# Two transformer blocks on one core: first loads spread out, masks made by GpSimd, memory norm one group later, two norms summed by halves

## The reference, cut to what matters

```python
for layer in range(2):                                   # first block
    h = rms_norm(x, norm_g[layer])
    sb_q, sb_k, sb_v, sb_g, mb_q, mb_k, mb_v, mb_g, mem_q, mem_g = split(h @ w_in[layer])
    o_sb  = stick_breaking_attention(...) * silu(sb_g)   # 6 heads
    o_mb  = softmax attention, causal, with rotary (...) * silu(mb_g)   # 6 heads
    m     = rms_norm(mem, mem_norm_g[layer])             # 256 memory rows of 1024
    mk, mv = split(m @ w_mem_kv[layer])
    o_mem = softmax(mem_q @ mk.T / 8) @ mv * silu(mem_g) # 4 heads
    x = x + concat(o_sb, o_mb, o_mem) @ w_out[layer]
x = rms_norm(x, final_norm_g)
# second block: 16 meta tokens in front of the 256
u = rms_norm(h, pre_mix_gain); proj = u @ w_in_2
merged = g_swa * (o_swa @ w_branch_swa) + g_diff * (o_diff @ w_branch_diff)
h = h + rms_norm(merged @ w_out_2, post_mix_gain)
u = rms_norm(h, pre_ffn_gain); gate, up = split(u @ w_ffn_in)
h = h + rms_norm((silu(gate) * up) @ w_ffn_out, post_ffn_gain)
```

## Time and profile before

| | |
|---|---|
| median of 3 runs | 888.32 us (886.84 to 890.65) |
| the profiled execution | 884.68 us, its span 882.9 us |
| PE busy | 829.7 us, 94% of the span |
| DVE, ACT, POOL busy | 554.1, 471.4, 122.4 us |
| mean granted clock of TensorE | 0.979 of full speed |
| transfers | 138.13 MB, 156 GB/s over the span |

### The profile page before, as it was taken

How to read it: one execution, slowest core, us unless ns; L and a number is a source line. 1 busy time by engine, 2 the same in 40 slices (tenths; PEclk the granted TensorE clock), 3 DMA queues, 4 the chain that set the end, 5 groups by cost and what they waited for, 6 DMA issues and landing times.

```text
span 882.9 us, 13033 instructions
## 1 busy us (share of the span) xinstructions
PE 829.7 (94%) x4350; PEld 684.0 (77%) x4350; DVE 554.1 (63%) x854; ACT 471.4 (53%) x962; POOL 122.4 (14%) x198
## 2 busy tenths in 40 slices
PE   7799999999999999699989999999998999999995
PEld 5678878777776787589878888888886788888884
DVE  5476667676777676756555665766566555455453
ACT  5476565375775554645555566555535544344343
POOL 0200121000232310153222524200000000000000
PEclk9999999999999999799999999999999899999999
DMA  9944543466676454652212434546664556656641
GB/s 268 268 139 128 146 120 122 141 177 205 193 216 184 139 161 120 174 143 83 63 55 71 127 108 126 166 145 208 204 202 138 186 182 193 209 155 197 207 137 48
DMA packets 147584, 138.13 MB, mean 156 GB/s; under 512 B 15184, under 2 KB 115680, under 8 KB 147520
## 3 DMA queue, kind: packets, MB, share of 16 engines
q1 hardware_dynamic: 145440, 130.21, 48.5%
q0 software_dynamic: 2080, 7.09, 2.8%
HBM read 136.22 MB, written 1.05 MB: 155 GB/s over the span
## 4 chain that ended last, share of the span: by engine, by line
PE 45%; ACT 4%; DVE 3%; issue 1%; ACTq 0%; DVEq 0%
PE psum L1059 38%; PE psum L1025 3%; PE psum L1142 2%; ACT probs L1406 2%; ACT w_hi L1294 1%; PE psum L1252 1%; DVE stats L1571 1%; DVE w_lo L1461 1%; PE psum L1255 1%; ACT xn L1316 0%; ACT gtmp L1436 0%; DVE xn L1500 0%; DVE x L1504 0%; ACT hstat L1439 0%; DVE o_st L1625 0%
## 5 line engine op out<-in xcount | busy, mean ns | idle before, releaser
L1461 DVE TENSOR_TENSOR w_lo<-raw,w_hi 128x1024 fp32r<-128x1024 f32 (+1 forms) x254 | 296.9, 1183 | 139.1 <-ACT w_hi L1294 82.3
L1294 ACT ACTIVATE w_hi<-raw 128x1024 fp32r<-128x1024 f32 (+1 forms) x254 | 253.0, 1015 | 70.7 <-PE psum L1059 47.2
L1059 PE MATMUL psum<-w_hi,h_hi 128*128 128x512 f32 (+1 forms) x656 | 262.8, 401 | 13.0 <-DVE h_lo L1510 10.3
L1059 PE MATMUL psum<-w_lo,h_hi 128*128 128x512 f32 (+1 forms) x656 | 248.8, 379 | 0.0
L1059 PE MATMUL psum<-w_hi,h_lo 128*128 128x512 f32 (+1 forms) x656 | 248.5, 379 | 0.0
L1059 PEld LDWEIGHTS psum<-w_hi,h_hi 128*128 128x128 f32 x656 | 125.7, 192 | 36.0 <-issue 15.8
L1059 PEld LDWEIGHTS psum<-w_lo,h_hi 128*128 128x128 f32 x656 | 125.1, 191 | 19.8
L1059 PEld LDWEIGHTS psum<-w_hi,h_lo 128*128 128x128 f32 x656 | 126.0, 192 | 16.2
L1406 ACT ACTIVATE probs<-psum,stats 128x272 f32<-128x272 f32 (+2 forms) x104 | 47.6, 467 | 87.4 <-DVE stats L1563 30.2
L1059 PE MATMUL psum<-w_hi,m_hi 128*128 128x512 f32 x152 | 60.0, 395 | 2.4 <-DVE m_lo L1510 1.7
L1059 PE MATMUL psum<-w_lo,m_hi 128*128 128x512 f32 x152 | 59.2, 390 | 0.0
(11 more groups left out here) (158 smaller groups left out, 1053.0 us busy)
## 6 DMA issues: line engine op xcount, KB each, us to landing
raw<-in_w_in SPq DMA_DIRECT2D x112, 256.0 KB, 3.5
raw<-in_w_in SPq DMA_DIRECT2D x44, 512.0 KB, 4.4
raw<-in_w_ffn_in SPq DMA_DIRECT2D x88, 256.0 KB, 3.9
raw<-in_w_out SPq DMA_DIRECT2D x24, 512.0 KB, 3.4
raw<-in_w_in SPq DMA_DIRECT2D x64, 192.0 KB, 2.7
raw<-in_w_ffn_out SPq DMA_DIRECT2D x22, 512.0 KB, 4.6
raw<-in_w_mem_kv SPq DMA_DIRECT2D x8, 512.0 KB, 3.8
raw<-in_w_branch_swa SPq DMA_DIRECT2D x8, 512.0 KB, 3.3
```

The costliest lines, as they stand in the source:

```text
L1059: last = nc.tensor.matmul(psum[:, bank, 0:n], sx[name][:, c, t * P:(t + 1) * P], wx[:, u["slot"], kk, 0:n], start=u["first"] and kk == 0 a ...
L1294: nc.scalar.activation(w_hi[:, u["slot"], :, 0:n], raw[:, u["raw"], :, 0:n], ACT.Copy)\
L1461: nc.vector.tensor_tensor(w_lo[:, u["slot"], :, 0:n], raw[:, u["raw"], :, 0:n], w_hi[:, u["slot"], :, 0:n].bitcast(F32), ALU.subtract)\
```

## The change

Five things change. First loads: the table `cf` is loaded in two other pieces (identity and triangle first, 128 KB; the rotary tables after unit 11 instead of unit 5, and with them no block of ones), the mask table is no longer loaded, GpSimd makes the masks from identity and triangle; its own loads (a gain, the memory rows in two halves, the small vectors, the next gain) wait for the 5th, 7th, 9th, 12th and 15th weight split, where before all of them waited for the 6th. Order of the groups: mb0 of layer 0 moves ahead of mkv and mem, with the memory norm beside it; `turn_mix` of the memory heads comes 9.75 units after their group instead of 11.5; `small` moves to layer 1. Between the blocks: the norm of the second token tile comes behind the transposes of the first. The two `addnorm`s: each bank is squared by itself (`half`), DVE multiplies it by the gain meanwhile, and the sum of the two halves gives the root; then one pass of DVE scales and adds. The diff, cut to its core:

```diff
-                out=(5.75, 6.75, 7.75, 8.75), turn_mix=(11.5,)),
+                out=(5.75, 6.75, 7.75, 8.75), turn_mix=(9.75,)),
...
-            side(head_group(layer, "sb", 1), {1: [("masks", None)], 3: [("small", None)]})
-            side(head_group(layer, "sb", 2), {0: mem_norm, 1: turns[:1], 2: turns[1:3], 3: turns[3:]})
+            side(head_group(layer, "sb", 1), {0: [("masks", None)]})
+            side(head_group(layer, "sb", 2), {})
+            side(head_group(layer, "mb", 0), {0: mem_norm, 1: turns[:1], 2: turns[1:3], 3: turns[3:]})
             turn_keys = memory_keys(layer, {})
             side(head_group(layer, "mem", 0), {0: [turn_keys]})
+            mem_norm, turns = memory_norm()
+            side(head_group(layer, "mb", 1), {0: mem_norm})
+            side(head_group(layer, "mb", 2), {k: [turn] for k, turn in enumerate(turns)})
...
-            side(meta_group(4), {0: [after[0], final[1]], 2: [after[1]]})
+            side(meta_group(4), {0: [after[0], final[1]]})
             line.extend(norm_turns("xn", "h", 0))
+            line.append(after[1])
...
-    tile_by_tile(a[2:] + b[2:], [post[0], pre[0]])
+    for t, name in enumerate(("unit_a", "unit_b")):
+        for g, units in zip(wo2, (a, b)):
+            line.extend((name, u) for u in units[2:])
+            line.append(half(post, g, t))
+        if t == 0:
+            line.extend([post[0], pre[0]])
     line.extend(norm_turns("xn", "h", 0) + [post[1]])
...
-            sp.dma_start(cf[:, 0:C_TRI], cf_dram[:, 0:C_TRI]).then_inc(s_ident, 16)
+            sp.dma_start(cf[:, 0:C_ONE], cf_dram[:, 0:C_ONE]).then_inc(s_ident, 16)
...
-                elif u["u"] == NRAW + 1:
-                    sp.dma_start(cf[:, C_TRI:C_END], cf_dram[:, C_TRI:C_END]).then_inc(s_const, 16)
-
-                    sp.dma_start(mask_in, cb_dram).then_inc(s_const, 16)
+                elif u["u"] == 11:
+                    sp.dma_start(cf[:, C_COS1:C_END], cf_dram[:, C_COS1:C_END]).then_inc(s_const, 16)
...
-            pool.wait_ge(hi_ready, NRAW + 2)
+            pool.wait_ge(s_ident, 16)
+            ident, below = cf[:, C_ID:C_ID + P], cf[:, C_TRI:C_TRI + P]
+            nc.gpsimd.memset(cf[:, C_ONE:C_ONE + P], -1.0)
+            nc.gpsimd.tensor_copy(cb[:, B_ID:B_ID + P], ident)
+            nc.gpsimd.tensor_scalar(cb[:, B_SB:B_SB + P], below, -NEG, None, ALU.mult)
+            nc.gpsimd.tensor_scalar(cb[:, B_LOW:B_LOW + P], below, NEG, NEG, ALU.mult, ALU.add)
+            link(nc.gpsimd.tensor_tensor(rtmp[:, 0, 0:P], below, ident, ALU.add))
+            nc.gpsimd.tensor_scalar(cb[:, B_UP:B_UP + P], rtmp[:, 0, 0:P], -NEG, None, ALU.mult)\
+                .then_inc(const_done, 1)
...
+            pool.wait_ge(hi_ready, 5)
             load_gain(pool, 1)
-            pool.dma_start(mem_v, A["mem"][0].rearrange("(t p) d -> p t d", p=P)).then_inc(s_mem, 16)
+            for t in range(NT):
+                pool.wait_ge(hi_ready, 7 + 2 * t)
+                pool.dma_start(mem_v[:, t, :], A["mem"][0, t * P:(t + 1) * P, :]).then_inc(s_mem, 16)
+            pool.wait_ge(hi_ready, 12)
...
-            pool.wait_ge(s_const, 32)
+            pool.wait_ge(hi_ready, 15)
+            pool.wait_ge(s_const, 16)
...
+                elif what == "half":
+                    g, t = s["g"], s["t"]
+                    wait(act, s["ready"])
+                    nc.scalar.activation(p_t[:, g["n"], :], psum[:, g["banks"][t], :], ACT.Square, scale=D ** -0.5,
+                                         accum_out=hsum[:, 2 * t + g["n"]:2 * t + g["n"] + 1]).then_inc(half_summed, 1)
+                elif what == "addnorm":
...
+                    link(nc.scalar.activation(more, more, ACT.Identity, bias=eps_col[:, :]))
+                    link(nc.scalar.activation(ss, ss, ACT.Ln, bias=more))
+                    nc.scalar.activation(rs, ss, ACT.Exp, scale=-0.5).then_inc(rstd_ready, 1)
...
-                elif what == "masks":
-                    dve.wait_ge(s_const, 32)
-                    nc.vector.tensor_copy(cb[:], mask_in).then_inc(const_done, 1)
...
+                elif what == "half":
+                    g, t = s["g"], s["t"]
+                    dve.wait_ge(*gain_use[i][1:])
+                    dve.wait_ge(half_summed, s["half"])
+                    at = slice(g["n"] * 512, (g["n"] + 1) * 512)
+                    link(nc.vector.tensor_tensor(xn[:, t, at], psum[:, g["banks"][t], :],
+                                                 gain[:, gain_use[i][0], at], ALU.mult))
+                elif what == "addnorm":
...
+                    nc.vector.scalar_tensor_tensor(out=x[:, t, :], in0=xn[:, t, :], scalar=nstat[:, 16 + c:17 + c],
+                                                   in1=x[:, t, :], op0=ALU.mult, op1=ALU.add).then_inc(norm_done, 1)
...
-                    if what == "addnorm":
-                        link(last)
-                        last = nc.vector.tensor_tensor(x[:, t, :], x[:, t, :], xn[:, t, :], ALU.add)
```

More of the change, by code:

```diff
@@ L118, in __init__ @@
                                     "his", "gated", "roped", "pts", "blends", "norms", "rstd", "norm_done",
-                                    "groups", "silus", "turns"), 0)
+                                    "groups", "silus", "turns", "halves"), 0)
     def next(self, name, n=1):
@@ L369, in number @@
                 outs_of_pt.append(s["o"] + 1)
+        elif what == "half":
+            s["ready"] = g["t_done"][s["t"]]
+            s["half"] = pl.next("halves")
         elif what in ("norm", "addnorm", "metanorm"):
@@ L374, in number @@
                 N["done"] = []
+            if what == "addnorm":
+                s["half"] = pl.count["halves"]
             if what == "metanorm":
                 s["ready"] = ("s_meta", 16)
-            elif what == "addnorm":
-                s["ready"] = product_done[t]
-            else:
+            elif what == "norm":
                 s["ready"] = (mem_ready if N["source"] == "mem" else x_ready)[t]
@@ L435, in norm_turns, with half @@
         return [("turn_norm", dict(source=source, dest=dest, t=t, c=c)) for c in range(0, KC, 4)]
-    def tile_by_tile(units, between=()):
-        line.extend(("unit_a", u) for u in units)
-        line.extend(between)
-        line.extend(("unit_b", u) for u in units)
+    def half(N, g, t):
+        return ("half", dict(norm=N[0][1]["norm"], g=g, t=t))
     w1 = [W["w_in"][layer] for layer in range(DEPTH)]
@@ L519, in make_plan @@
             with_meta(head_group(layer, "mem", 0, (0, 1)), 2, {0: [("rope_meta", dict(n=1))]})
-        for p in range(3):
-            extra = {}
-            if layer == 0 and p == 0:
-                mem_norm, turns = memory_norm()
-                extra = {0: mem_norm}
-            elif layer == 0 and p == 1:
-                extra = {k: [turn] for k, turn in enumerate(turns)}
-            if layer == 1 and p == 0:
-                with_meta(head_group(layer, "mb", p, (0, 1)), 3, {0: [("rope_meta", dict(n=2))]})
-            elif layer == 1:
-                side(head_group(layer, "mb", p, (2, 3) if p == 1 else (0, 1)), extra)
-            else:
-                side(head_group(layer, "mb", p), extra)
+            with_meta(head_group(layer, "mb", 0, (0, 1)), 3, {0: [("rope_meta", dict(n=2))]})
+            side(head_group(layer, "mb", 1, (2, 3)), {0: [("small", None)]})
+            side(head_group(layer, "mb", 2, (0, 1)), {})
         outs = [pl.group("wo", banks() if layer == 0 else ((2, 3), (0, 1))[n], units_of(
@@ L633, in make_plan @@
     last_outs = outs_of(nf - 1)
-    line.extend(("unit_a", u) for u in last_outs)
     final = norm("addnorm")
-    line.append(final[0])
-    line.extend(("unit_b", u) for u in held + last_outs)
-    line.append(final[1])
+    for t, name in enumerate(("unit_a", "unit_b")):
+        if t:
+            line.extend((name, u) for u in held)
+        for g, u in zip(fo, last_outs):
+            line.extend([(name, u), half(final, g, t)])
+        line.append(final[t])
     pl.steps = lay_out(line)
@@ L793, in build @@
         for i, (what, s) in enumerate(STEPS):
-            if what in ("norm", "metanorm", "addnorm") and s["t"] > 0:
+            if what in ("norm", "metanorm", "addnorm", "half") and "gain" in s["norm"]:
                 gain_use[i] = s["norm"]["gain"]
@@ L797, in build @@
                 continue
-            if what in ("norm", "metanorm", "addnorm") or (what == "evac" and s["g"]["kind"] == "gates"
+            if what in ("norm", "metanorm", "half") or (what == "evac" and s["g"]["kind"] == "gates"
                                                           and s["g"]["n"] % 2 == 0 and s["t"] == 0):
@@ L1301, in _ @@
                     split(s)
[L1302 removed]
+                elif what == "half":
[4 more added lines that the diff above has]
+                elif what == "addnorm":
+                    N, t = s["norm"], s["t"]
+                    c = 4 * (N["n"] % 4) + 2 * t
```

(6 more changed lines are left out.)

50 lines of the change are left out of this document (19 added, 31 removed).

## The result

The changed kernel takes 882.16 us (median of 18 runs, 880.32 to 887.23), the kernel before 888.38 (18 runs). The ratio is 0.9948 with a 95% interval of 0.9929 to 0.9968: 2.8 to 6.3 us less. Forecast were 882.5 us. Timed once more beside later experiments (e5), it took 881.92 against 888.51, ratio 0.9932 (0.9911 to 0.9953).

The account below looks back on a forecast made before the run. PE, busy 94% of the span, was taken as the bound, so other engines cost only where PE waits. Terms summed to -5.84 us, from 888.32 to 882.5; the 8-in-10 range was 878.8 to 888.8.

Parts of the forecast that it names:

- Start: Up to the first matmul: larger first table costs 0.25 us, GpSimd's masks beside `w_lo` 0.1, together +0.35.
- Mask wait: PE's wait for `cb` near 32 us goes, since GpSimd makes the masks long before: -1.62 us.
- late weights: PE's 3.10 us wait at 43.46: 0.73 MB less in GpSimd's loads lets weights arrive earlier, -2.7 us.
- Low clock at 44 us: Behind the wait at 43.46, 4 us at clock 0.61 should stay high without that wait: -1.56 us.
- Between the blocks: PE's 5.09 us wait for the first `h_lo` shortens as the second tile's norm moves behind it: -1.3 us.
- After `w_out_2`: Wait for `xn` falls to 0.8 us, but the second tile's multiplications delay `h_lo`: +0.1 in all.
- End: The shortened norm chain behind the last matmul, exposed with only the store after it: -1.4 us.
- the starvation moves forward: Rival, 890.4 us, chance 0.07: three early 0.52 MB GpSimd loads hold up SP's weights, 5.9 us together.
- The weights stay late: Rival, 886.8 us, chance 0.17: the savings of 2.7 and 1.56 us do not come.
- Each new wait brings a low clock: Rival, 885.6 us, chance 0.16: (a) and (b) cost 2 x 1.56 us more.
- (a): Layer 0, memory keys' transposes: PE waits until DVE has read a bank of the two-bank ring, +0.6 us.
- (b): Layer 0, memory heads' output transposes right ahead of the unit needing their `mix` parts: PE waits, +1.69 us.

Follow-up runs that it names:

- e5: The changed kernel once more, unchanged, timed beside e6 and e7: 881.92 us against 888.51 for the kernel before, ratio 0.9932.
- e8: Changed kernel with the mask table again, loaded by SP and cast by DVE, GpSimd's loads still spread: 887.57 us, ratio 1.0011 to the kernel before.
- e2: Changed kernel with all of GpSimd's loads issued behind the 6th weight split again, masks still by GpSimd: 891.32 us, ratio 1.0018 to the kernel before.
- e6: Changed kernel with GpSimd's large loads (gain, memory rows) behind the 6th weight split, small vectors still behind the 12th: 883.35 us, ratio 0.9949.
- e7: Changed kernel with only the small vectors moved ahead, behind the 6th weight split: 886.99 us, ratio 0.9984 to the kernel before.
- e3: Changed kernel with the second tile's halves at `w_out_2` behind the first tile's `h_hi` and `h_lo`: 878.56 us, ratio 0.9891.
- e9: Kernel before with one edit, small vectors and the gain behind them waiting for the 12th weight split instead of the 6th: 881.92 us, ratio 0.9944.

## Why the prediction was right

The time was forecast to 0.3 us by nine terms. Six came out singly (start, both new waits of layer 0, the chain between the blocks, `w_out_2`, end), two only as a sum and for a wrong cause, and the ninth, the low clock, can't be read from one pair of traces. So the closeness of the total is in part luck.

- *Start, +0.35*: in the first pair of traces the first matmul came at 12.01 instead of 12.07, as if nothing were lost. Over all traces it came at 11.92 to 12.13 in ten with the larger table, and at 12.07, 11.34 and 11.62 in the three with the smaller one, on average 0.36 later. Masks on GpSimd are not the reason, as e8, which makes none there, starts at 12.06. The loss that I allowed for beside `w_lo` had hardly a place to come from: the last mask step ends at 10.06, 0.03 us after the first `w_lo` begins (0.25 in e5), and that `w_lo` takes the 1.23 us that it took before:

```profile
9.53 0.53 POOL L907 TENSOR_SCALAR cb<-rtmp 128x128 bf16<-128x128 f32 x1
10.03 1.23 DVE L1472 TENSOR_TENSOR w_lo<-raw,w_hi 128x1024 fp32r<-128x1024 f32 x1 [2.26 <-ACT w_hi L1294]
```

- *Mask wait, -1.62, and late weights, -2.7*: the sum of -4.3 was right (the first `sbt` matmul came 4.8 earlier), the parts were wrong. They are not two terms: e2 keeps one edit and PE waits 6.20, e8 keeps the other and PE waits 4.13. The cause was wrong too. "0.73 MB less at 268 GB/s" took bytes for the price; e6 moves 1.57 MB for 1.4 us, e7 0.2 MB for 5.1. That the step gave the right figure is luck: the 0.73 MB that I took out of the stretch are the small vectors (0.2) and a gain (0.52), and I priced every byte alike, where the 0.2 did most of it.
- *Low clock at 44 us, -1.56*: gone in both traces of after. But I took one trace's low stretches as given. They come behind other waits in other runs, so the term is a mean over runs; from 10 and 13 to 9 and 9 it is 2.5 x 1.7 = 4.3 us, an upper bound, since some of these stretches lie where PE waits anyway.
- *Layer 0, +0.6 and +1.69*: 0.77 and 1.50 measured. I did not see the 0.39 for a row of the memory norm, nor the 0.18 more at 72 us.
- *Between the blocks, -1.3*: from the start of the last matmul of the meta tokens to the first unit it took 6.06 us instead of 7.45 in the first pair of traces, 6.03 instead of 7.45 in the second. The wait itself shows only 5.09 to 4.45 in the first pair, because the transposes ahead of it ran at the higher clock after the change (1.06 us instead of 1.82 for the eight); in the second pair, at 1.06 both times, it shows 5.84 to 4.45. What I left out is that the matmuls behind the wait can be slower by the clock: there 0.5 of the 1.4 went again on average (5.26 to 5.76 us to the next transposes).
- *After `w_out_2`, +0.1*: 0.85 and 3.37 were measured, 0.8 and 3.4 forecast; the first unit of the FFN came 0.1 later after the last `w_out_2` matmul (5.27 against 5.17). e3 shows that the halves were the reason.
- *End, -1.4*: from the last wait for `m_lo` to the end of the span 14.5 us in both traces instead of 15.8 and 15.9.
- *Layer 1, 0*: the table shows none lost or won in it. The one new wait is 0.48 us for `o_st` at 289 (0.56 in e5); that for `x` at its start, 0.72 and 0.75 in the traces of before, is 1.45 and 1.01.

Of the rivals, "the starvation moves forward" had its mechanism: the units at 28 and 31 us are later in the changed kernel. It had no effect because GpSimd makes the masks, which e8 shows by taking that away. "The weights stay late" is e2. None of the rivals had the small vectors, on which most of the gain hangs (e7, e9). "Each new wait brings a low clock" did not hold at (a) and (b); the low stretch of 129 us lies behind an old wait.

The Trainium skill names small pieces as slow ("DMA: Bandwidth & Descriptors", section "Why small descriptors are slow (HBM only)"): by its account a fixed cost comes with each piece, 27% at 256 bytes. The runs agree in direction, but the factor of six in e6 and e7 is far above it. Why the small vectors cost that much more stays open.

## What to carry to other kernels

A load is to be costed by the share of the DMA engines that its packets hold, and not by its bytes: look at the queue's packets, MB and share in the stretch where the rate falls though the engines are busy. Two waits that stand behind one late transfer are one term; undo each edit alone before crediting it. A step that shortens a chain pays only if nothing that it adds stands ahead of the next instruction for which the bottleneck waits (PE's wait shrank by 1.5 us in e3 by exchanging two steps).

## What the runs showed of the hardware

- Small vectors (rows of 64 to 512 bytes) spread over 128 partitions by GpSimd's queue: in e7 0.19 MB held 88.5% of 16 DMA engines for 3 us. In the kernel before, the rate of all transfers fell from 401 to 144 GB/s as they passed, other loads of the queue among them. A gain with rows of 4 KB, spread in the same way, moved 0.30 MB for each us of all engines against 0.07.
- The low clock behind a wait of PE comes in some executions and not in others: 4 to 14 such stretches of about 1.7 us each in a trace, behind waits of 1 to 6 us. The waits that stayed, such as those of 1.78 before the `qk` transposes near 445 us, had one behind them in nearly every trace, those of 2.1 to 2.3 near 55 to 80 us in some.
- Six GpSimd steps of 128x128 made the masks between 6.98 and 10.06 us, before the first `w_lo` ran, so they tell nothing of GpSimd beside `w_lo`. The kernel before does: the pair of `w_lo` at 110.60 us lost 0.14, and it was GpSimd that lost more. One of its steps, first ahead of that pair and then beside it (times on GpSimd are rough):

```profile
109.82 0.24 POOL L995 TENSOR_TENSOR rtmp<-stage,cf 128x32 f32<-128x32 f32 x1
111.96 1.23 POOL L995 TENSOR_TENSOR rtmp<-stage,cf 128x32 f32<-128x32 f32 x1
```
